# The last block of a five-block transformer kernel: VectorE's order, ScalarE's copies, TensorE's transposes and half waits

## What is computed

```python
h = rms_norm_2(x, g_norm1[l]) * (1.0 + scale1) + shift1
proj = h @ w_in[l]
na_q, na_k, na_v, q_lat, kv_lat, k_rot, gate_na, gate_mla = jnp.split(proj, split_at, axis=-1)

qa = rms_norm_2(na_q.reshape(B, S, NA_HEADS, NA_HEAD_DIM), g_na_q[l])
ka = rms_norm_2(na_k.reshape(B, S, NA_HEADS, NA_HEAD_DIM), g_na_k[l])
y_na = neighbourhood_attention(qa, ka, va, na_rpb[l])

qm = (rms_norm_2(q_lat, g_q_lat[l]) @ w_uq[l]).reshape(B, S, MLA_HEADS, MLA_QK_DIM)
q_nope, q_rope = qm[..., :MLA_NOPE_DIM], apply_rope(qm[..., MLA_NOPE_DIM:], positions)
kvm = (rms_norm_2(kv_lat, g_kv_lat[l]) @ w_ukv[l]).reshape(B, S, MLA_HEADS, MLA_NOPE_DIM + MLA_V_DIM)
k_nope, vm = kvm[..., :MLA_NOPE_DIM], kvm[..., MLA_NOPE_DIM:]
qm = rms_norm_2(jnp.concatenate([q_nope, q_rope], axis=-1), g_mla_q[l])
km = rms_norm_2(jnp.concatenate([k_nope, k_rope], axis=-1), g_mla_k[l])
y_mla = blocked_full_attention(qm, km, vm)
merged = (jax.nn.sigmoid(gate_na) * (y_na @ w_proj_na[l]) + jax.nn.sigmoid(gate_mla) * (y_mla @ w_proj_mla[l]))
x = x + gate1 * (merged @ w_out[l])
```

## Time and profile before

| what | value |
|---|---|
| median of 3 runs | 1475.25 us (1474.83 to 1476.41) |
| the profiled execution's own time | 1473.68 us |
| its span (first to last instruction) | 1471.9 us |
| TensorE busy | 1339.8 us (91%) |
| VectorE busy | 674.8 us (46%) |
| ScalarE busy | 420.3 us (29%) |
| GpSimd busy | 101.5 us (7%) |
| mean granted clock of TensorE | 0.956 of full speed |

### The profile page before, as it was taken

One profiled execution on the slowest core, in us unless ns is written; L12 is line 12 of the kernel. 1 busy time (PEld: TensorE's weight loads), 2 busy tenths in 40 slices (PEclk: granted clock), 3 DMA queues, 4 the chain that ended last, 5 costly groups with the idle time before them and its releaser, 6 DMA issues. The chain is left out here.

```text
span 1471.9 us, 18731 instructions
## 1 busy us (share of the span) xinstructions
PE 1339.8 (91%) x7184; PEld 907.3 (62%) x7184; DVE 674.8 (46%) x1459; ACT 420.3 (29%) x786; POOL 101.5 (7%) x131
## 2 busy tenths in 40 slices
PE   5998989999899799995987969997999999999997
PEld 5887755897469557995665558544544544444444
DVE  4575664656465436524367765336122222222223
ACT  4251533435244324315243125101111111111111
POOL 1221041000500000000101100000000000000000
PEclk9989999999899999987999889998999999999999
DMA  8543543657155615453035331301999999999991
GB/s 320 175 172 115 184 162 114 218 197 280 36 200 186 229 46 183 172 178 56 0 129 193 114 115 59 114 10 34 422 422 421 422 422 421 422 421 406 412 405 43
DMA packets 105298, 317.54 MB, mean 216 GB/s; under 512 B 15633, under 2 KB 21009, under 8 KB 84113
## 3 DMA queue, kind: packets, MB, share of 16 engines
q1 hardware_dynamic: 102208, 312.56, 55.8%
q10 hardware_dynamic: 3026, 4.11, 0.8%
HBM read 315.60 MB, written 1.05 MB: 215 GB/s over the span
## 5 line engine op out<-in xcount | busy, mean ns | idle before, releaser
L1320 ACT ACTIVATE weights_high<-ring 128x2048 fp32r<-128x2048 f32 (+2 forms) x78 | 141.4, 1862 | 230.7 <-PE psum L649 66.0
L1710 DVE TENSOR_TENSOR weights_low<-ring,weights_high 128x2048 fp32r<-128x2048 f32 (+2 forms) x78 | 171.7, 2239 | 38.1 <-ACT weights_high L1320 37.4
L649 PE MATMUL psum<-input_high,weights_high 128*128 128x256 f32 x480 | 137.9, 287 | 7.0 <-DVEq L1749 6.2
L649 PE MATMUL psum<-input_high,weights_low 128*128 128x256 f32 x480 | 137.3, 286 | 0.0
L649 PE MATMUL psum<-input_low,weights_high 128*128 128x256 f32 x480 | 137.3, 286 | 0.0
L668 PE MATMUL psum<-ring,uT 128*128 128x512 f32 x304 | 133.3, 599 | 0.9 <-DVEq L1680 0.9
L660 PE MATMUL psum<-weights_high,input_high 128*128 128x512 f32 (+2 forms) x272 | 102.3, 376 | 6.8 <-issue 4.8
L668 PEld LDWEIGHTS psum<-ring,uT 128*128 128x128 f32 x304 | 58.2, 193 | 72.0 <-issue 70.9
L2522 DVE TENSOR_TENSOR y_low<-psum,y_high 128x512 fp32r<-128x512 f32 x54 | 36.0, 689 | 144.2 <-ACT y_high L1535 144.2
L1118 PE MATMUL psum<-gate_up0b,V 128*64 128x512 f32 x224 | 101.5, 596 | 0.0
L1118 PE MATMUL psum<-gate_up0a,V 128*64 128x512 f32 x224 | 101.5, 596 | 0.0
(11 more groups left out here) (376 smaller groups left out, 2568.7 us busy)
## 6 DMA issues: line engine op xcount, KB each, us to landing
gate_up0a<-in_exp_gate_up SPq DMA_DIRECT2D x28, 1024.0 KB, 12.5
gate_up0b<-in_exp_gate_up SPq DMA_DIRECT2D x28, 1024.0 KB, 14.4
gate_up1a<-in_exp_gate_up SPq DMA_DIRECT2D x26, 1024.0 KB, 11.8
gate_up1b<-in_exp_gate_up SPq DMA_DIRECT2D x26, 1024.0 KB, 13.7
ring<-in_w_ada SPq DMA_DIRECT2D x12, 2048.0 KB, 8.2
ring<-in_b_w_in SPq DMA_DIRECT2D x8, 2048.0 KB, 8.7
ring<-in_d_w_in SPq DMA_DIRECT2D x8, 2048.0 KB, 8.8
ring<-in_a_w_in SPq DMA_DIRECT2D x7, 2048.0 KB, 8.8
```

Source lines behind the costliest of these rows:

```text
L649: last = nc.tensor.matmul(bank[:, 256 * f:256 * f + 256], w2_[x][:, d, col + 128 * f:col + 128 * f + 128], in2[y][:, d, :], start=(k == 0) ...
L1320: nc.scalar.activation(w_hi[m % 2][:, x], ring[i][:, x], ACT.Copy).then_inc(s_wh, 1)
L1710: v.tensor_tensor(w_lo[i][:, x], ring[i][:, x], w_hi[m % 2][:, x], ALU.subtract).then_inc(s_wl, 1)
```

## The change

- **Half waits.** A new helper `low_half` waits for the first half of a low part before slice 0 and for the second before slice 4. `proj` uses it in all forms, in every layer.
- **Opening of E.** The transposes of the second tile stand at slice 2 of W1 instead of 4.
- **Latents' transposes** move from behind W3 to between W2 and W3.
- **ScalarE takes out** both fills of gate rows, both of MQ, and W4, W5, W6 with the sigmoid in the same instruction (`acc_out_of`). The pairs are waited for through ScalarE's semaphores.
- **Transposes in the middle of blocks.** NQ behind W4, NK in the middle of W5, the first half of MQ behind W5, its second in the middle of W6, the first half of MK behind W6, its second in the middle of W7.
- **VectorE's order** is written anew for this, and the scratch of the 96-wide head sums is `gpost` instead of `QK`.

```diff
+            def low_half(lows, d):
+                if lows is not None and d % 4 == 0:
+                    pe.wait_ge(s_wl, lows - (d == 0))
...
-            def proj(kind, n=512):
+            def proj(kind, n=512, releaser="d", between=None):
...
-                pe.wait_ge(s_wl, 2 * m)
-                a, b = acc("d")
+                a, b = acc(releaser)
...
-                    mm_P(a[:, 0:n], w, 0, 0, n)
+                    mm_P(a[:, 0:n], w, 0, 0, n, lows=2 * m)
+                    if between is not None:
+                        between()
                     last = mm_P(b[:, 0:n], w, 1, 0, n)
...
-            opening(416)
-            proj("RR")
+            opening(416, at=2)
             proj("RR")
             pe.wait_ge(s_u, c.up("u"))
             transposes(LAT, CH[0:3])
+            proj("RR")
             gate_rows()
...
-            proj("RR")
-            proj("RR")
+            MH = [(96 * k, 96) for k in range(8)]
+            proj("RR", releaser="a")
             pe.wait_ge(s_u, c.up("u"))
             transposes(NQ, CH[0:4])
-            transposes(NK, CH[0:4])
-            proj("RR")
-            transposes(MQ, [(96 * k, 96) for k in range(8)])
-            transposes(MK, [(96 * k, 96) for k in range(8)])
-            attention(UN + UM, FULL, 64, "RR", (4,))
+            proj("RR", releaser="a", between=lambda: transposes(NK, CH[0:4]))
+            pe.wait_ge(s_u, c.up("u"))
+            transposes(MQ, MH[0:4])
+            proj("RR", releaser="a", between=lambda: transposes(MQ, MH[4:8]))
+            pe.wait_ge(s_u, c.up("u"))
+            transposes(MK, MH[0:4])
+            attention(UN + UM, FULL, 64, ("RR", 512, "d", lambda: transposes(MK, MH[4:8])), (4,))
...
+            def acc_out_of(fill, kind, dst0, dst1, n=512):
+                act.wait_ge(acc_done, fill + 1)
+                i = fill % 2
+                nc.scalar.activation(dst0, banks[2 * i][:, 0:n], kind)
+                nc.scalar.activation(dst1, banks[2 * i + 1][:, 0:n], kind).then_inc(free["a", i], 1)
```

More of the change, by code:

```diff
@@ L483, in build, with out_by_act @@
         acc_router = fills_of(STREAM)
+        ON_ACT = [acc_E + k for k in (4, 5, 6, 7, 10, 11, 12)] + [acc_M + k for k in range(4)] + [acc_router]
+        def out_by_act(fill):
+            return free["a", fill % 2], sum(k <= fill and k % 2 == fill % 2 for k in ON_ACT)
         SPLITS, at, fills, loaded = [], 0, 0, [0] * RING
@@ L647, in mm_T @@
                     for d in range(DC):
+                        low_half(lows if f == 0 else None, d)
                         for y, x in PARTS:
@@ L725, in half_P, with opening @@
                 return last
-            def opening(n=512, n_=512):
+            def opening(n=512, n_=512, at=DC // 2):
                 lows, w = split_block(n)
@@ L805, in attention @@
                     unit_scores(units[n])
-                proj(last_block)
+                proj(*last_block)
                 for n in range(len(units)):
@@ L949, in _ @@
                 last.then_inc(o_done, 1)
-            attention(UA, CAUSAL, 64, "TR", (8,), MODS_A)
+            attention(UA, CAUSAL, 64, ("TR",), (8,), MODS_A)
             project_out(u)
@@ L955, in _ @@
                 proj(kind)
-            attention(UB, CAUSAL, 128, "RR", (1, 4), MODS_B)
+            attention(UB, CAUSAL, 128, ("RR",), (1, 4), MODS_B)
             project_out(u)
@@ L1040, in _ @@
             for t in range(T):
-                a, b = acc("d")
+                a, b = acc("a")
                 for bk, at in ((a, 0), (b, 384)):
@@ L1494, in _ @@
             next_layer(3)
-            w_high(6)
-            funcs(do_sigmoid, z[:, :, :], z[:, :, :])
-            funcs(do_sigmoid, u[:, :, 0:512], u[:, :, 0:512])
+            w_high(3)
+            for n, base in ((4, 2 * D), (5, 5 * D)):
+                acc_out_of(acc_E + n, ACT.Copy, mod[:, base:base + 512], mod[:, base + 512:base + 1024])
+            for t in range(T):
+                acc_out_of(acc_E + 6 + t, ACT.Copy, MQ[:, t, 0:384], MQ[:, t, 384:768], 384)
+            w_high(2)
+            acc_out_of(acc_E + 10, ACT.Sigmoid, z[:, 0, 0:512], z[:, 1, 0:512])
+            w_high()
+            acc_out_of(acc_E + 11, ACT.Sigmoid, z[:, 0, 512:1024], z[:, 1, 512:1024])
+            acc_out_of(acc_E + 12, ACT.Sigmoid, u[:, 0, 0:512], u[:, 1, 0:512])
             c.tr += 14
@@ L1749, in input_low, with evac @@
                 dve.sem_inc(s_uT, 1)
-            def evac(dst0, dst1, n=512, scale=None):
+            def evac(dst0, dst1, n=512, scale=None, low=True):
                 a, b, f = acc_in()
@@ L1756, in evac @@
                 last.then_inc(f, 1)
-                next_low()
+                if low:
+                    next_low()
             def flat(ap):
@@ L2293, in rope, with queries_keys_in @@
                     own()
+            qr = [MQ[:, t, :].rearrange("p (h n) -> p h n", n=96)[:, :, 64:96] for t in range(T)]
+            def queries_keys_in(dst, n, gains):
+                tr_in(dst, n, gains)
+                tr_own()
             evac(LAT[:, 0, :], LAT[:, 1, :], n=416)
@@ L2378, in _ @@
                 tile_in(uT, t)
-            for _ in range(3):
-                act_does()
+            act_does()
+            for k in (11, 12):
+                dve.wait_ge(*out_by_act(acc_E + k))
             for t in range(T):
@@ L2405, in _ @@
             pair = acc_router % 2
-            dve.wait_ge(free["a", pair], len(UM) // 2 + 1)
+            dve.wait_ge(*out_by_act(acc_router))
             sc = gate[:, :, 0:64]
```

80 lines of the change are left out of this document (39 added, 41 removed).

## The result

The kernel after takes 1441.73 us (median of 4 runs, 1439.6 to 1444.71), the kernel before 1475.3 beside it on the same chip: a ratio of 0.9773, 95% interval 0.9751 to 0.9795. That is 33.6 us less, where 31.2 were forecast, and inside the range. The profiled execution of after is the slowest of the four, 1444.71 us with a span of 1442.6, so profile against profile the gain is 29.0 us (1473.68 - 1444.71). Two executions of the experiments, one of `weights_split_wait` (4619.97 us) and one of `opening_in_middle` (1941.77 us), were slow ones and are in no median, ratio or count.

A forecast was written before the change was run, and what follows sets the result against it. TensorE bounds the kernel almost everywhere; in E's projections it waits, mostly for VectorE. Terms 3.6 + 1.2 + 1.4 + 16.1 + 8.9 = 31.2 us, from the median 1475.25 to 1444.1 us, range 1438.5 to 1451.5.

The forecast's parts named there:

- Part 1: First `proj` of layers B to E: half waits remove four gaps, 4.8 us, 3.6 in B to D, 1.2 in E.
- Part 2: Opening of E: transposes come 6 matmuls sooner, the wait of 2.66 us becomes 1.3; 1.4 us gained.
- Part 3: Gate rows and up projections in E: shorter waits and full clock, 16.1 us gained.
- Part 4: Transposes in the middle of E's blocks: 14.3 us gone, less 4.1 of waits and 1.3 of low clock, 8.9 gained.
- P: W4's start in block E, from which VectorE's order was followed; forecast at 808.9.
- the low clock: Behind the new wait at MQ's transposes in E: TensorE at 1.2 GHz costs 1.3 us, bounds 0 and 2.7.
- VectorE slips further: Rival, E from W4 to NK's banks: VectorE 5% later and W6's first half at 1.2 GHz, 1449.6 us; 18 in 100.
- No new wait: Rival, E's MQ transposes: VectorE's work overlaps better, 4.1 and 1.3 us come back, 1438.7 us; 6 in 100.
- ScalarE copies at a third of VectorE's speed: Rival, E's gate fills and MQ: 2.05 us a copy, last pair 7 us late, 1451 us; 2 in 100.
- The load of W4: Rival, E: late DMA holds ScalarE's high part ahead of the gates' copies, some 5 us late, 1449; 5 in 100.
- The slow case: Rival, E: TensorE stays at 1.2 GHz from the new wait to W7's end, 1472 us; 3 in 100.
- 29 to 30 us: Sign of being right: W7 ends some 29 to 30 us earlier within E.

The follow-up runs named there:

- weights_split_wait: Kernel after with NK's transposes taken out ahead of W6's low part and that part's first half moved ahead of MQ's scaling; 1439.64 us, repeated 1439.61.
- opening_in_middle: Kernel after with the second tile's transposes in block E's opening behind four slices again, not two; 1443.22 us.
- after_again: Kernel after, unchanged, run again on one chip beside repeats of two other kernels; 1444.73 us, ratio to before 0.9779.
- vector_2us_more: Kernel after with two more unused squares of MK on VectorE ahead of MK's sums; 1444.37 us.
- nk_out_first: Kernel after with VectorE taking NK's transposes out ahead of W6's low part instead of behind it; 1438.18 us, repeated 1437.93.
- low_ahead_of_sums: Kernel after with VectorE taking NK out, then W6's low part, then MK's sums, MQ's taking out split around MK's scaling; 1442.6 us.
- halves_alone: Kernel before with the half waits only; 1464.85 us, ratio to before 0.9941.

## Why the prediction was right

**Part 1, half waits (4.8).** The mechanism was right: all four gaps are gone. The size was low in B, C and D and high in E. The step that failed is the reading of a wait's length as its price: the runs showed 1.4 to 1.5 us for each 1.20 in the three layers, and 0.4 for E's 1.16 in the kernel after. The forecast of 3.6 for layers A to D, against 2.1 in the profile of after, failed in appearance only: the profile of after comes to layer B's opening at 248.74 us and that of before at 246.03, 2.7 us earlier, over code of layer A in which the change removes nothing (2.0 of it in the output projection, in the table of the last section). From there to W0 after is 4.85 us ahead.

**Part 2 (1.4).** The wait fell from 2.66 to 1.30, as forecast. From W0 to W2 after is 24.09 us long and before 26.83: 2.74, where part 2 and E's half wait were priced at 2.6.

**Part 3 (16.1).** From W2 to W4 it was 51.52 us and is 35.38: 16.14. The single terms hold as well: V's wait 0.36 (0.3 forecast), the second fill 1.98 (1.88), 5.32 for the up projections (5.3). Here a trace of before was enough, because the new order has no queue in it that was close. The rule of the Trainium skill ("ScalarE: Activation LUTs", Rules for kernel authors), that such plain work belongs on VectorE, did not fit these float32 tiles out of PSUM (the page gives its factor for bf16): ScalarE's copies of 512 columns took 0.60 us here too (the rows are below), and VectorE's 0.68 to 0.69 of the same tiles in before. The two are nearly equal. What giving them back to VectorE cost, 7.6 us in E, was not their own length but their place in VectorE's queue: TensorE waited 5.15 us for them.

```profile
798.14 0.60 ACT L1374 ACTIVATE mod<-psum 128x512 f32<-128x512 f32 x1 [1.26 <-PE psum L906]
798.64 0.59 ACT L1375 ACTIVATE mod<-psum 128x512 f32<-128x512 f32 x1
```

**Part 4 (8.9).** From W4 to W7's end it was 66.87 us and is 58.81: 8.1. The new wait came where it was foretold, with its length: MQ's transposes start 27.7 us behind P where P + 27.4 was worked out, a wait of 3.85 for 3.7. VectorE's walk is off by 0.3 us over 26. The step that failed is the low clock: 1.3 was taken, 2.9 measured (0.9 in the transposes, 2.0 in W6's first half), which is just above the upper bound of 2.7. I took the value from a wait of 3.43 us in a stretch of other work; the nearer row was that of the up projections, where the bound came from, and it fits (2.7). The rest of the part came out 0.8 us better than its sum; that a wait's price is more than its bracket, as in part 1, points that way, but no run splits the 0.8. That the part as a whole came within 0.8 us is therefore in part luck, two errors of opposite sign. So is the low clock itself: the same wait gave 2.9, 2.9 and 2.0 us in after, `after_again` and `opening_in_middle`, and the longer one of `vector_2us_more` 2.0.

**The rivals.** "VectorE slips further" did not come: VectorE was 0.3 us late. "No new wait" did not come by itself. `nk_out_first` comes to its time, 1438.2 and 1437.9 where the rival said 1438.7, but still has a wait of 1.78 us. `weights_split_wait` has no wait from W4 to the scores, and its E is 6.2 us shorter than that of after where the rival takes 5.4 away; its medians are 1439.6 both times. "ScalarE copies at a third of VectorE's speed" did not come, at 0.60 us a copy (its 3 x 0.65 is 1.95, not 2.05, which changes nothing). The load of W4 did not hold ScalarE: its high part began at 791.33 and was done at 795.04, before the first gate at 795.80. The slow case did not come: the low clock ended within W6's first half (its matmuls are 0.23 us apart again from 840.08 on).

**The sum.** In E 27.6 forecast, 26.94 measured (the "29 to 30 us" among the signs does not follow from the forecast's own terms, which give 27.6); the halves in A to D 3.6 forecast, 4.5 in the stages that hold them; behind E nothing and nothing. Of the 2.4 us by which the median beat the forecast, 0.2 is in these (0.9 more in the halves, 0.7 less in E); the rest is no more than what stages that the change does not touch move by (the table in the last section), and the second comparison, with 1444.73, lies on the forecast's other side.

## What to carry to other kernels

- Walk the engine that everything waits for through its new order, instruction by instruction, from one fixed point P. It found a wait of 3.7 us that stood in no trace yet, to 0.2 us, and named the instruction to move.
- When that engine has hardly a pause left, another order moves the wait, and is worth what the new wait is shorter (1.78 us in `nk_out_first`, 3.29 in `low_ahead_of_sums`); to be rid of it, fill a pause or give work away (`weights_split_wait`, ScalarE's copies).
- Compare stretches that repeat to 0.1 us (here W0's start to W7's end) before comparing medians, and take a wait's price from two starts, not from the idle time in brackets: 1.20 in brackets was 1.4 to 1.5.

## What the runs showed of the hardware that I had not expected

**The same wait, another clock.** Start to start of the same rows in layers A to C and behind E, in profiled executions of kernels that have the same code in these stages and the same waits to a few tenths:

| stage | before | halves_alone | after | nk_out_first | after_again |
|---|---|---|---|---|---|
| A, attention, from its wait of 2.49 us on | 54.76 | 57.69 | 54.82 | 54.66 | 57.85 |
| A, output projection | 39.41 | 39.36 | 41.40 | 39.37 | 41.14 |
| B, output projection, from a wait of 4.0 us on | 42.20 | 41.24 | 42.24 | 41.21 | 42.13 |
| C, from the scores of 494 us to the attention's end | 28.31 | 26.62 | 27.94 | 26.62 | 27.65 |
| output projection behind E, from its wait of 2.46 us on | 35.09 | 35.08 | 35.09 | 36.55 | 35.09 |

Each stage has two to four values, 1 to 3 us apart between the ends, and they do not go with the kernel. The rows of A, in `before` and in `halves_alone`, show where the first 3 us are:

```profile
145.83 1.54 PE L793 MATMUL psum<-ident,probs 128*128 128x128 f32 x6 [2.49 <-ACT probs L1361]
147.16 2.66 PE L771 MATMUL psum<-V,probsT 128*128 128x64 f32 x12
...
152.62 1.45 PE L771 MATMUL psum<-V,probsT 128*128 128x64 f32 x12
154.00 0.71 PE L760 MATMUL psum<-QK 64*128 64x256 f32 x4
```

```profile
144.31 1.54 PE L799 MATMUL psum<-ident,probs 128*128 128x128 f32 x6 [2.49 <-ACT probs L1367]
145.65 2.66 PE L777 MATMUL psum<-V,probsT 128*128 128x64 f32 x12
...
151.17 2.66 PE L777 MATMUL psum<-V,probsT 128*128 128x64 f32 x12
153.76 1.23 PE L766 MATMUL psum<-QK 64*128 64x256 f32 x4
```

Behind the same wait of 2.49 us both run at the low clock (2.66 us for 12 matmuls that take 1.45). In the first the matmuls are at full speed again by 152.62, some 7 us behind the wait, in the second they are still slow at 153.76, 9 us behind it. What decides between them no run here shows; the pieces of work are the same. The differences are large enough for the spread of one kernel's runs over 4 to 7 us (1438.74 to 1445.39 for after), and they are why an edit worth 1.4 us can't be read from medians of five runs.

**GpSimd is held while VectorE makes a low part.** In the rows of POOL in the section on the result, the first operation on MQ's sums takes 0.20 us and the one on MK's 2.36; the second takes 2.89 and 4.81. The slow pair starts at 828.79, together with VectorE's low part (4.49 for two halves, so the first ends at about 831.1 and the second at 833.3). 828.79 + 2.36 is 831.15, and 833.3 + 2.9 is 836.2, where the second ends at 836.04. So it looks as if an operation that starts during a half waits for its end, then takes its usual time. The openings of the layers show the same, in before too. In layer B of after an operation that takes 0.22 us elsewhere takes 0.94 and ends with the half, at 248.67 and 248.59:

```profile
247.73 0.94 POOL L1617 TENSOR_SCALAR small<-small 128x1 f32<-128x1 f32 x1 [3.92 <-ACT QK L1304]
```

```profile
246.31 2.28 DVE L1746 TENSOR_TENSOR weights_low<-ring,weights_high 128x2048 fp32r<-128x2048 f32 x1
```

In `nk_out_first` the roots of MK start beside a taking out of transposes and no low part, and take 0.21 and 2.90 us again. One that has started is not disturbed: in `weights_split_wait` GpSimd's row and VectorE's overlap, and both keep their length.

```profile
816.14 2.90 POOL L1628 TENSOR_TENSOR small<-small 128x16 f32<-128x16 f32 x1
```

```profile
817.55 2.29 DVE L1746 TENSOR_TENSOR weights_low<-ring,weights_high 128x2048 fp32r<-128x2048 f32 x1
```

The Trainium skill ("GPSIMD Engine Reference", Specifications) names the two engines' shared way to SBUF and says that they contend when an instruction of VectorE has two SBUF inputs; a low part has, so the trace agrees. That it holds the start and not the course is my reading of these places; no run was made to test it, but `nk_out_first`, made for another reason, moves the low part away and the 2.36 and 4.81 us go. It cost nothing here but 1.22 us of VectorE's time after 834.9, ahead of MK's scaling, which TensorE did not wait for.
